# A hybrid decoder step on one core: the V rows of a half step stand behind one half step more of mixer items in TensorE's order

## The chip, the core and the metric

The kernel is one program on one core of a Trainium2 chip. Five engines run at once, each through its own list of instructions in program order, and meet only at semaphores: PE (TensorE, matrix products), DVE (VectorE), ACT (ScalarE), POOL (GpSimd, which here only issues gathers once the recurrence is over) and SP (SyncE, which issues weight loads). The metric is the device time of one execution in microseconds (us), median of the runs.

## The reference

One decoder layer for 512 prompt tokens and 64 sample tokens (8 sequences of 8), width 1024, all float32:

```python
z = x @ w_in + b_in;  u, q, k, v, g_ssm, g_attn = split(z)
y = s5_scan(u, ...);  ga, gb = split(gelu(y) @ w_glu + b_glu);  ssm_branch = ga * sigmoid(gb)
attn_branch = window_attention(rope(q), rope(k), v, sinks) @ w_attn_up
mix = (sigmoid(g_ssm) * ssm_branch + sigmoid(g_attn) * attn_branch) @ w_out
x1 = layer_norm(ALPHA * x + mix)
# PEER: 8 heads, each picks 16 of 16384 experts for every token
h = einsum('nhkd,nd->nhk', peer_u[idx], x1);  a = gelu(h) * gate
x2 = layer_norm(ALPHA * x1 + einsum('nhk,nhkd->nd', a, peer_v[idx]))
```

For each token 128 rows of `peer_u` and 128 rows of `peer_v`, 4 KB each, are fetched from HBM.

## The kernel before, in words

**Tiles.** The tokens are five tiles: tile 0 holds the 64 sample tokens, tiles 1 to 4 hold 128 prompt tokens each. They pass through the expert layer in the order 1, 0, 2, 3, 4 (`ORDER`). A *slot* (t, k) of a tile is one expert choice of all its tokens: one gather of 128 U rows and one of 128 V rows, 512 KB each. Tiles 1 to 4 have 128 slots; tile 0 is folded on 128 partitions and has 64. A *half step* is two slots, the item `("peer", t, c)`, with slots 2c and 2c+1.

**What a slot passes through.** POOL gathers the U row (L663) into a ring; DVE multiplies it with the token and sums (the *dot*, L1462); after four dots ACT applies gelu (L1762), DVE multiplies by the gate (L1431), and ACT makes a diagonal matrix of the four columns (L1754). The V row has been gathered by POOL meanwhile (L672), four slots behind the U row, and is added to the tile's sum either by PE (two matmuls of 512 columns with the diagonal as weights, L1001, four records in the trace) or, for some slots that a planner picks (`rows_on_vector`), by DVE (L1450). The V rows that `("peer", t, c)` uses are 2c-4 and 2c-3.

**What waits for what.** POOL issues in one list: U row q, V row q-4, U row q+1, and so on. Slots are counted through over tiles here (q). A U row waits until the dot of the earlier holder of its place is done, a V row until the earlier holder of its place has been added (`wait_v_used`). For the first 72 slots the V ring has 9 places, from there to the end of tile 0 it has 6 (`V_PLACES`): V row q then waits for V row q-6. Since the list is in order, a V row that waits also holds back all U rows behind it.

**The mixer beside it.** While tiles 1 and 0 are in their slots, the token mixer of tiles 2 to 4 runs in small items between the half steps: `qkv`, `turn`, `s`, `pt`, `pv` (attention), `gs`, `ga` (gates: 8 matmuls with K of 128 each, L896), `merge` (gb, gl and up: 16 such matmuls), `wo` (4 matmuls each, L924), `wo_last` (L934), `xt` (transposes of the normed tile, L944), `wq` (the expert queries, L953) and `sc` (L984). `schedule()` writes out one list of all items; every engine walks it in a version of its own. DVE's and ACT's versions put their share of the mixer items one or two half steps behind (`half_steps_behind`). PE's version is `mixer_first`: it holds each `peer` item back behind the mixer items that follow it, until the next `peer` or `last` item comes.

`rows_on_vector` walks the same two versions with a table of costs, to choose which V rows DVE adds; so the function has two uses.

Of the kernel before, what the change touches and what calls it, by code (L numbers as in the profile page):

```python
# [28 lines left out]
ORDER = [1, 0, 2, 3, 4]  # L29
# [138 lines left out]

def mixer_first(items):


    out, held = [], None
    for item in items:
        if item[0] in ("peer", "last") and held:
            out.append(held)
            held = None
        if item[0] == "peer":
            held = item
        else:
            out.append(item)  # L180
    return out + ([held] if held else [])


def half_steps_behind(items, lag):
# [25 lines left out]
def rows_on_vector(items):  # L210
# [3 lines left out]
    for engine, order in enumerate((half_steps_behind(items, VECTOR_BEHIND), mixer_first(items))):  # L214
        sums, n = [0.0] * (len(steps) + 1), -1 + engine
        for item in order:
            if item[0] == "peer" and item[1] not in ORDER[:2]:
                break
            if item[0] == "peer":
                n += 1  # L220
            elif n >= engine:
                sums[min(n, len(steps))] += COST.get(item[0], (0, 0))[engine]
        load.append(sums)
# [114 lines left out]
def hybrid_step(nc, io):  # L338
# [12 lines left out]
    with ctx:  # L351
# [334 lines left out]
        def _(pe):  # L686
# [334 lines left out]
            for item in mixer_first(plan.items):  # L1021
                if item[0] in here:
                    here[item[0]](*item[1:])
# [866 lines left out]
```

## Time and profile before

| | |
|---|---|
| median of 3 runs | 2079.44 us (2075.89 to 2082.87) |
| the profiled execution, its own time | 2086.46 us |
| its span, first to last instruction | 2084.6 us |
| PE busy | 1600.2 us (77%) |
| DVE busy | 1301.2 us (62%) |
| ACT busy | 442.6 us (21%) |
| POOL busy | 1237.5 us (59%) |
| mean granted TensorE clock | 0.880 |
| HBM | 323 GB/s over the span |

The slots of tile 1 run from 285 us to about 735 us of the span, those of tile 0 from there to about 957 us, those of tiles 2 to 4 take the rest. "Idle before" in a row is the time in which the engine did nothing just before that instruction, and the name behind the arrow is what ended it. A PE row at half clock takes about twice as long. A busy share is an average; which engine holds up a stretch is read from who waits there.

### The profile page before, as it was taken

What the parts mean: (1) busy time and instruction counts of PE and PEld (TensorE: products, weight loads), DVE (VectorE), ACT (ScalarE), POOL (GpSimd) and SP (SyncE); (2) the same over time, 40 slices, a digit from 0 to 9 for tenths busy, and PEclk for the clock granted to TensorE, in tenths of its full rate; (3) what the DMA queues carried; (4) which work ended last, traced back from release to release, by engine and by line L of the source; (5) the groups of instructions that cost most, each with busy time, mean ns of one, the idle gap of its engine ahead of it and who ended that gap; (6) DMA issues with size and microseconds to landing.
All of it is one profiled execution on the core that took longest, in us unless ns stands there. A gap on an engine that the chain in (4) does not pass through costs nothing.

```text
span 2084.6 us, 16770 instructions
## 1 busy us (share of the span) xinstructions
PE 1600.2 (77%) x4829; PEld 811.7 (39%) x4829; DVE 1301.2 (62%) x3093; ACT 442.6 (21%) x1035; POOL 1237.5 (59%) x1370
## 2 busy tenths in 40 slices
PE   7999969798997987974777767577658765777766
PEld 5796655354553432421332323232223322222222
DVE  7820258888888777585786658365758535544345
ACT  2332212354332311111121102111112111111111
POOL 1181027675677657577566667656666675666664
PEclk9999979899998998987888889888888877898987
DMA  6352359997999989899899999989999998999997
GB/s 220 104 156 78 121 209 327 393 342 269 345 405 410 365 329 346 300 351 380 322 342 367 370 371 371 376 313 383 354 368 375 355 393 323 350 369 372 383 377 273
DMA packets 186699, 675.08 MB, mean 324 GB/s; under 512 B 20976, under 2 KB 23456, under 8 KB 186192
## 3 DMA queue, kind: packets, MB, share of 16 engines
q0 software_dynamic: 167056, 609.25, 77.7%
q1 hardware_dynamic: 17632, 59.51, 8.0%
q10 hardware_dynamic: 1920, 5.24, 0.7%
q8 instruction: 40, 0.66, 0.1%
q14 instruction: 51, 0.42, 0.1%
HBM read 669.71 MB, written 3.69 MB: 323 GB/s over the span
## 4 chain that ended last, share of the span: by engine, by line
PE 33%; DVE 20%; POOL 16%; issue 13%; another core or an unknown queue 9%; DMA 7%; ACT 2%; ACTq 0%; POOLq 0%; DVEq 0%; SPq 0%
PE bank L1001 14%; POOL region L672 5%; DVE wring L1462 4%; PE bank L896 4%; POOL region L663 4%; DVE region L1462 4%; POOL wring L663 4%; PE first_banks L896 2%; DMA region<-in_pu,region 2%; DMA wring<-in_pu,region 2%; DMA region<-in_pv,region 2%; PE bank L806 1%; PE bank L713 1%; PE first_banks L806 1%
## 5 line engine op out<-in xcount | busy, mean ns | idle before, releaser
L1001 PE MATMUL bank<-region,small 128*128 128x512 f32 (+1 forms) x1380 | 693.3, 654 | 260.1 <-ACT small L1754 124.0
L672 POOL DMA_INDIRECT region<-in_pv,region x392 | 397.3, 1014 | 250.6 <-issue 104.2
L1001 PEld LDWEIGHTS bank<-region,small 128*128 128x128 f32 (+1 forms) x1380 | 272.4, 204 | 658.2 <-issue 557.8
L663 POOL DMA_INDIRECT region<-in_pu,region x298 | 310.7, 1043 | 194.3 <-issue 84.7
L663 POOL DMA_INDIRECT wring<-in_pu,region x278 | 276.4, 994 | 107.7 <-issue 78.0
L1462 DVE CUSTOM_DVE_ANT_0 wring<-wring,first_banks 128x1024 f32<-128x1024 f32 x228 | 271.7, 1218 | 107.5 <-DMA wring<-in_pu,region 83.0
L1754 ACT ACTIVATE small<-small,region 128x128 f32<-128x128 f32 (+1 forms) x503 | 169.0, 389 | 644.8 <-remote 201.3
L1462 DVE CUSTOM_DVE_ANT_0 region<-region,first_banks 128x1024 f32<-128x1024 f32 x156 | 186.8, 1218 | 72.2 <-DMA region<-in_pu,region 59.9
L1462 DVE CUSTOM_DVE_ANT_0 region<-region 128x1024 f32<-128x1024 f32 x142 | 171.6, 1225 | 38.0 <-DMA region<-in_pu,region 36.5
L1001 PE MATMUL bank<-discretisation,small 128*128 128x512 f32 (+1 forms) x200 | 117.3, 714 | 91.3 <-ACT small L1754 63.3
L1762 ACT ACTIVATE region<-region 128x4 f32<-128x4 f32 x144 | 29.2, 203 | 519.2 <-DVE region L1462 294.6
L1001 PE MATMUL bank<-wring,small 128*128 128x512 f32 x252 | 120.3, 617 | 14.2 <-issue 9.5
L1431 DVE TENSOR_TENSOR region<-region 128x4 f32<-128x4 f32 x144 | 23.1, 161 | 127.6 <-issue 66.1
L1001 PEld LDWEIGHTS bank<-discretisation,small 128*128 128x128 f32 (+1 forms) x200 | 40.2, 213 | 155.0 <-issue 115.8
L1001 PE MATMUL bank<-small 128*128 128x512 f32 (+1 forms) x180 | 93.4, 644 | 7.4 <-issue 6.2
L672 POOL DMA_INDIRECT discretisation<-in_pv,region x60 | 67.1, 1119 | 45.9 <-issue 24.1
L672 POOL DMA_INDIRECT wring<-in_pv,region x64 | 62.2, 971 | 32.6 <-issue 18.8
L1001 PEld LDWEIGHTS bank<-wring,small 128*128 128x128 f32 x252 | 48.4, 197 | 82.4 <-issue 82.0
L1450 DVE SCALAR_TENSOR_TENSOR region<-region 128x1024 f32<-128x1024 f32 x45 | 57.9, 1287 | 33.6 <-issue 25.3
L896 PE MATMUL bank<-xT,wring 128*128 128x192 f32 (+1 forms) x336 | 77.2, 388 | 0.0
L672 POOL DMA_INDIRECT small<-in_pv,region x60 | 61.4, 1023 | 23.2 <-issue 21.8
L1462 DVE CUSTOM_DVE_ANT_0 wring<-wring,region 128x1024 f32<-128x1024 f32 x50 | 60.8, 1222 | 21.3 <-DMA wring<-in_pu,region 20.9
(343 smaller groups left out, 1964.8 us busy)
## 6 DMA issues: line engine op xcount, KB each, us to landing
wring<-in_w SPq DMA_DIRECT2D x100, 512.0 KB, 5.0
region<-in_pv,region POOLq DMA_INDIRECT x392
region<-in_pu,region POOLq DMA_INDIRECT x298
wring<-in_pu,region POOLq DMA_INDIRECT x278
region<-in_w SPq DMA_DIRECT2D x4, 512.0 KB, 6.5
small<-in_small ACTq DMA_DIRECT2D x1, 1669.0 KB, 9.0
xT<-in_xT SPq DMA_DIRECT2D x1, 1536.0 KB, 13.6
region<-in_x SPq DMA_DIRECT2D x3, 512.0 KB
```

The source lines that it names most:

```text
L663: pool.indirect_dma_start(ring_u[u_at.place[q]], None, io["pu"], bass.IndirectOffsetOnAxis(ind[:, k:k + 1], 0)).then_inc(g_u[u_at.place[q] ...
L672: pool.indirect_dma_start(ring_v[v_at.place[q]], None, io["pv"], bass.IndirectOffsetOnAxis(ind[:, k:k + 1], 0)).then_inc(g_v[v_at.place[q] ...
L713: last = mm(b[:, 0:cn], w[:, k, :], xT[:, k, c0:c0 + cn], start=k == 0, stop=k == KT - 1)
L806: last = mm(b[0:tn, 0:n], xT[:, k, t0:t0 + tn], w[:, k % kp, :], start=k == 0, stop=k == KT - 1)
L896: last = mm(b[:, 0:cn], w[:, k0 + k, :], src[:, k, s0:s0 + cn], start=k == 0, stop=k == kn - 1)
L1001: last = mm(bank[6 + hf][0:tn, :], diag[:, d % DIAGS, 0:tn], ring_v[v_at.place[q]][:, 512 * hf:512 * hf + 512], start=k == 0, stop=t > 1 a ...
L1431: V.tensor_tensor(aact[:, n % 2, k], hact[:, n % 2, k], gt[:, k], ALU.mult).then_inc(a_s, 1)
L1450: V.scalar_tensor_tensor(out=acc, in0=ring_v[v_at.place[q]], scalar=aact[:, n % 2, k:k + 1], in1=acc, op0=ALU.mult, op1=ALU.add).then_inc( ...
L1462: V.tensor_tensor_reduce(out=ring_u[u_at.place[q]], in0=ring_u[u_at.place[q]], in1=first_banks[:, :] if t > 1 else x1[t], scale=1.0, scala ...
L1754: S.activation(diag[:, d % DIAGS, 0:tn], eye, ACT.Copy, scale=aact[:, n % 2, k:k + 1]).then_inc(diag_s, 1)
L1762: S.activation(hact[:, n % 2, k], hdot[:, n % 2, k], ACT.Gelu).then_inc(act_s, 1)
```

## The change

`mixer_first` now holds back up to two `peer` items in tiles 1 and 0 (`ORDER[:2]`) instead of one, so that the V rows of half step c stand behind the mixer items of half step c+1 as well. At a `last` item both held ones come out, and from tile 2 on the rule is the old one. No item is added or taken away.

```diff
-    out, held = [], None
-    for item in items:
-        if item[0] in ("peer", "last") and held:
-            out.append(held)
-            held = None
+    out, held = [], []
+    for n, item in enumerate(items):
         if item[0] == "peer":
-            held = item
+            if len(held) == (2 if item[1] in ORDER[:2] else 1):
+                out.append(held.pop(0))
+            held.append(item)
+            while len(held) > 1 and item[1] not in ORDER[:2]:
+                out.append(held.pop(0))
+        elif item[0] == "last":
+            out += held + [item]
+            held = []
         else:
             out.append(item)
-    return out + ([held] if held else [])
+    return out + held
```

The planner's choice moves with it: DVE adds 41 rows of tile 1 instead of 39 (in the first 64 slots rows 3, 7, 11, 12, 13 and 17 instead of 8, 9, 14 and 15; rows 72 and 73 go to PE, 70, 78, 80, 81, 96 and 97 among others to DVE) and 29 of tile 0 instead of 30 (rows 14, 15 and 30 come to DVE, rows 13, 16, 42 and 43 go to PE). The rest of the kernel is the same, 3 lines further down.

PE's list where tile 0 begins its slots, before. L924 is `wo`: rows 1 to 3 of this piece are `wo(0)` (4 matmuls), L1001 with 64x512 is V row (0, 0), and what follows is `wo(1)` and the beginning of `wo(2)`.

```order
L924 MATMUL first_banks<-wring,region 128x512
L924 MATMUL bank<-wring,region 128x512 x2
L924 MATMUL first_banks<-wring,region 128x512
L1001 MATMUL bank<-region,small 64x512 x2
L924 MATMUL first_banks<-wring,region 128x512
L924 MATMUL bank<-wring,region 128x512 x2
L924 MATMUL first_banks<-wring,region 128x512 x2
```

The same place in the changed kernel (L924 is L927 there, L1001 is L1004):

```order
L927 MATMUL first_banks<-wring,region 128x512
L927 MATMUL bank<-wring,region 128x512 x2
L927 MATMUL first_banks<-wring,region 128x512 x2
L927 MATMUL bank<-wring,region 128x512 x2
L927 MATMUL first_banks<-wring,region 128x512
L1004 MATMUL bank<-region,small 64x512 x2
L927 MATMUL first_banks<-wring,region 128x512
```

V row (0, 0) has moved from behind `wo(0)` to behind `wo(1)`, four matmuls later.

PE's list in the middle of tile 0, before: `xt(2)` (L944), V rows 20 and 21, `xt(3)`, rows 22 and 23, `xt(4)`, rows 24 and 25, `wq(1, 0)` (L953), rows 26 and 27.

```order
L944 MATMUL bank<-small,region 128x128 x4
L944 MATMUL first_banks<-small,region 128x128 x4
L1001 MATMUL bank<-discretisation,small 64x512 x2
L1001 MATMUL bank<-small 64x512 x2
L944 MATMUL first_banks<-small,region 128x128 x4
L944 MATMUL bank<-small,region 128x128 x4
L1001 MATMUL bank<-region,small 64x512 x4
L944 MATMUL bank<-small,region 128x128 x4
L944 MATMUL first_banks<-small,region 128x128 x4
L1001 MATMUL bank<-region,small 64x512 x4
L953 MATMUL first_banks<-xT,wring 128x384 x8
```

The same place in the changed kernel (L944 is L947, L953 is L956): `xt(2)`, rows 18 and 19, `xt(3)`, rows 20 and 21, `xt(4)`, rows 22 and 23, `wq(1, 0)`, rows 24 and 25.

```order
L947 MATMUL bank<-small,region 128x128 x4
L947 MATMUL first_banks<-small,region 128x128 x4
L1004 MATMUL bank<-region,small 64x512 x4
L947 MATMUL first_banks<-small,region 128x128 x4
L947 MATMUL bank<-small,region 128x128 x4
L1004 MATMUL bank<-discretisation,small 64x512 x2
L1004 MATMUL bank<-small 64x512 x2
L947 MATMUL bank<-small,region 128x128 x4
L947 MATMUL first_banks<-small,region 128x128 x4
L1004 MATMUL bank<-region,small 64x512 x4
L956 MATMUL first_banks<-xT,wring 128x384 x8
L1004 MATMUL bank<-region,small 64x512 x4
```

Each pair of rows has moved behind one `xt` or `wq` item more: rows 20 and 21 now stand behind `xt(3)`, rows 22 and 23 behind `xt(4)`.

## Rows read from the trace of the kernel before

**Rows 1.** Busy time by stretch: all engines, clock, DMA share, GB/s

```profile
500.00:730.00 230.00, 210.88 (x600) 112.94 (x600) 184.84 (x394) 74.87 (x114) 155.26 (x136) 0.96 0.96 370
730.00:960.00 230.00, 184.95 (x452) 77.19 (x452) 163.13 (x289) 39.47 (x90) 150.24 (x129) 0.90 0.91 332
```

**Rows 2.** Waits of POOL, 285 to 956 us: total, times, longest

```profile
POOL region L672 <- PE bank L1001: 64.7, 20, 15.4
...
POOL region L663 <- DVE region L1462: 28.3, 8, 6.7
```

**Rows 3.** Timeline of PE: last attention item, then the first gate

```profile
500.99 1.93 PE L883 MATMUL first_banks<-region 128*64 128x128 f32 x16 [2.22 <-ACT region L1521]
...
506.39 5.32 PE L896 MATMUL first_banks<-xT,wring 128*128 128x384 f32 x16
```

**Rows 4.** Waits of DVE, 285 to 956 us, on attention items

```profile
DVE region L1253 <- PE bank L873: 7.9, 1, 7.9
...
DVE region L1253 <- PE first_banks L883: 4.2, 1, 4.2
```

**Rows 5.** The page's groups: a V row added by DVE

```profile
L1450 DVE SCALAR_TENSOR_TENSOR region<-region 128x1024 f32<-128x1024 f32 x45 | 57.9, 1287 | 33.6 <-issue 25.3 <-DMA region<-in_pv,region 7.2 <-DVE region L1431 0.4
```

**Rows 6.** Timeline of PE: V rows 74 and 75 of tile 1

```profile
569.96 3.60 PE L1001 MATMUL bank<-region,small 128*128 128x512 f32 x8
```

**Rows 7.** Timeline of POOL: V row 80 and U row 85 issued

```profile
572.12 1.34 POOL L672 DMA_INDIRECT region<-in_pv,region  x1 [3.60 <-PE bank L1001]
573.76 0.94 POOL L663 DMA_INDIRECT region<-in_pu,region  x1 [0.31 <-issue]
```

**Rows 8.** Timeline of DVE: the dot of slot 85

```profile
583.03 1.22 DVE L1462 CUSTOM_DVE_ANT_0 region<-region 128x1024 f32<-128x1024 f32 x1 [3.08 <-DMA region<-in_pu,region]
```

**Rows 9.** Timeline of PE: its stalls late in tile 1

```profile
632.60 5.37 PE L1001 MATMUL bank<-region,small 128*128 128x512 f32 x8 [4.04 <-ACT small L1754]
...
655.96 5.62 PE L1001 MATMUL bank<-region,small 128*128 128x512 f32 x8 [5.96 <-DMA region<-in_pv,region]
...
678.90 6.11 PE L1001 MATMUL bank<-region,small 128*128 128x512 f32 x8 [4.42 <-ACT small L1754]
```

**Rows 10.** Timeline of PE: wo(0), V row (0, 0), wo(1)

```profile
756.72 2.08 PE L924 MATMUL first_banks<-wring,region 128*128 128x512 f32 x2 [6.06 <-DVE region L1283]
...
763.10 1.93 PE L1001 MATMUL bank<-region,small 128*64 128x512 f32 x4
764.96 1.12 PE L924 MATMUL first_banks<-wring,region 128*128 128x512 f32 x2
765.92 1.88 PE L924 MATMUL bank<-wring,region 128*128 128x512 f32 x4
```

**Rows 11.** Timeline of POOL: V row 6 of tile 0

```profile
765.30 0.94 POOL L672 DMA_INDIRECT region<-in_pv,region  x1 [15.41 <-PE bank L1001]
```

**Rows 12.** Timeline of PE: xt(3), rows 22 and 23, xt(4), rows 24 and 25, wq(1, 0)

```profile
831.20 1.09 PE L944 MATMUL first_banks<-small,region 128*128 128x128 f32 x4 [7.68 <-DVE region L1311]
...
833.07 5.77 PE L1001 MATMUL bank<-region,small 128*64 128x512 f32 x8
843.33 0.66 PE L944 MATMUL bank<-small,region 128*128 128x128 f32 x4 [4.49 <-DVE region L1305]
...
844.44 5.21 PE L1001 MATMUL bank<-region,small 128*64 128x512 f32 x8
849.58 5.43 PE L953 MATMUL first_banks<-xT,wring 128*128 128x384 f32 x16
```

**Rows 13.** Timeline of POOL: V rows 28, 30, 34, 36 and 37 of tile 0

```profile
837.01 0.94 POOL L672 DMA_INDIRECT region<-in_pv,region  x1 [4.50 <-PE bank L1001]
...
848.21 1.27 POOL L672 DMA_INDIRECT region<-in_pv,region  x1 [5.44 <-PE bank L1001]
...
866.08 0.94 POOL L672 DMA_INDIRECT region<-in_pv,region  x1 [3.83 <-PE bank L1001]
...
875.01 0.94 POOL L672 DMA_INDIRECT region<-in_pv,region  x1 [4.06 <-PE bank L1001]
...
878.55 0.95 POOL L672 DMA_INDIRECT region<-in_pv,region  x1 [0.30 <-issue]
```

## The prediction

> **What bounds the kernel now.** The change reaches only tiles 1 and 0, the stretch from 285 to about 957 us. I read the busy time by stretch first. From 500 to 730 us PE is busy 211 of 230 us and the DMA engines 0.96 of the time; from 730 to 960 us both are looser, 185 us and 0.91 [rows 1]. So neither is simply the bound. The waits of POOL tell more, since POOL's one list of gathers feeds the whole expert layer: in this part it stood 64.7 us, 20 times, for V rows that PE had not yet added (in one destination buffer alone), against 28.3 us for dots of DVE [rows 2]. The reader is to see that PE's V rows, the very thing that the change moves later, already hold POOL back more than anything else does. Then I followed single places in the timelines: where PE stalls on a diagonal with a mixer item behind it, and where POOL stalls on a V row with a mixer item ahead of it. The first kind gains by the change, the second loses.
>
> **The change part by part.** PE's work is the same: the same matmuls, two or three V rows fewer. What differs is when a V row is added. In a stretch where PE runs without a gap, the mixer items keep their times, and each pair of V rows stands one mixer item later, 5.3 us for a gate [rows 3]. What this costs is read in four places.
>
> *Attention of tile 1, up to 506 us.* Two effects of opposite sign. DVE waited 7.9 and 4.2 us for attention items of PE [rows 4]; with a pair of rows (3.6 us) less ahead of them they could come up to 3.6 us earlier each, 7 us in all. But the last of these items waited itself for ACT's copy, 2.2 us [rows 3], so there the order of PE gives nothing. Against it, DVE adds 6 of the first 64 rows instead of 4, at 1.29 us each [rows 5], and DVE is nearly always busy there: 2.6 us. Bounds: -7 to +5 us (the 2.6 us doubled, if the later rows are late for DVE as well). I take 0, between the ends, since the only one of the two waits whose cause is plain is the one that cannot shrink.
>
> *The stretch without a gap, 506 to 628 us.* At V row 74 the 6-deep ring closes: V row 80 stood 3.6 us until row 74 was added, at 571.8 [rows 7], PE having begun it at 569.96 right behind a `merge` [rows 6]. In the changed list rows 72 and 73 (now on PE, 3.6 us) and the gate `gs(1, 2)` (5.3 us) stand ahead of it: it is added at 569.96 + 3.6 + 5.3 + 1.7 = 580.5, so V row 80 goes out 8.3 to 8.7 us later. U row 85 is the next in POOL's list, and DVE was waiting for just this row: issued at 573.76, its dot begun at 583.03 after 3.08 us of waiting for the landing [rows 7, 8]. So the dots from there on come up to 8.3 us later. PE does not feel it yet, since its own use of the rows is later too. From 628 us on PE has stalls of 4.0, 6.0 and 4.4 us [rows 9]; these it can now fill with mixer items, ACT gets its mixer results sooner and stands less in the way of the diagonals. That gives back something of the 8.3 us, but not what the gathers lost while the DMA engines are 0.96 busy [rows 1]. Bounds 0 and 8.3 us; I take 4, the middle, because the giving back hangs on ACT, which no row here prices.
>
> *Tile 0 begins.* POOL stood 15.4 us until V row (0, 0) was added, then issued V row 6 at 765.30 [rows 11]. PE had done `wo(0)` from 756.72 (after a wait for DVE that the change doesn't touch) and row (0, 0) at 763.10 [rows 10]. Now `wo(1)` comes between. Its four matmuls lie where rows 764.96 and 765.92 begin them: two records by 765.92, four more of 1.88 us and two more, 3.5 us in sum. Everything in POOL's list is behind this, and DVE has run dry: **+3.5 us**. If PE is at half clock there, as it was for `wo(0)`, 7 us; nothing below 3.4.
>
> *The middle of tile 0.* PE reached `xt(3)` at 831.2 after 7.7 us of waiting for DVE, and `xt(4)` at 843.3 after 4.5 us [rows 12]; rows 20 and 21 had been done ahead of the first wait, rows 22 and 23 ahead of the second. Now each pair stands behind it. Counted in the times of before: `xt(4)` ends at 844.4; rows 22 and 23 take 5.2 us at the clock of that moment (as the pair at 844.44 did), `wq(1, 0)` 5.4, rows 24 and 25 3.6, `wq(1, 1)` 5.4, rows 26 and 27 3.6, `wq(1, 2)` 5.4, row 28 1.8: added at 874.8. V row 34 waits for it and was issued at 866.08, 8.7 us earlier [rows 13]. V row 28 goes out at 848 instead of 837.01, V row 30 at 857 instead of 848.21. Row 30 is added by DVE now, so V row 36 no longer waits for PE and comes at POOL's own pace, four gathers of 1.25 us (0.94 and 0.31 between two [rows 7]) behind V row 34: 880 against 875.01. V row 37 waits for row 31, behind row 29, `wq(1, 3)` and its own 1.8 us: 874.8 + 1.8 + 5.4 + 1.8 = 883.8 against 878.55. From there no gather waits for PE. **+5.3 us** stays. Bounds: 0, if the dots of DVE had room for it, and 9, if row 30 doesn't help.
>
> *What is given back.* 53 gathers of tile 0 are left behind V row 37. POOL's mean for one is 1.165 us from 730 to 960 us (150.24 us by 129) [rows 1], while many take 0.94 [rows 7]; at best it regains 0.22 x 53 = 12 us. It would do so only if DVE worked less beside it, and DVE has the same dots and rows to do, later. I take 1 us. A rule of the Trainium skill bears on this (SBUF — State Buffer, section Who interferes with whom): a DVE instruction with two inputs in SBUF blocks a GpSimd instruction that reads SBUF, the later one waiting for the whole of the first. By it a POOL that had been held up, with DVE run dry, would gather at 0.94 us and more of the loss would come back.
>
> The sum is 0 + 4 + 3.5 + 5.3 - 1 = 11.8 us. Tiles 2 to 4 have the old order and shift as a whole; tile 2 begins behind the last gather of tile 0. On the profiled execution, 2086.46 us, this makes 2098.3; that execution lies 7.0 us above the median of the runs, so on the median it is 2079.44 + 11.8 = **2091.3 us**.
>
> **The rivals.**
>
> *Faster: the stalls of PE are filled.* Mechanism: from 628 us on, PE waits with ready mixer items behind it; the three stalls sum to 14.4 us [rows 9]. If the end of tile 1 follows from PE's mixer items, and the loss at row 74 finds slack, 14.4 us come off there, and the losses of tile 0 (8.8 us) are paid from them only in part, if `xt` and `wo` come earlier as well: about 2079.4 - 9 = 2070. It decides once the mixer chain, not the gathers, is what DVE waits for after 628 us. For it: PE's busy 211 of 230 us. Against it: each of these stalls ended on a diagonal or a V landing, so the gathers were behind PE, not PE behind them. A rule of the skill speaks for this rival (Perfetto Trace Analysis, section Optimization Strategies): where the matmul engine idles for others, one should work on keeping it going. Taken as a rule for this kernel it would give the 14.4 us.
>
> *No difference.* The V rows have room: the delays at 572 us and in the middle of tile 0 are swallowed by later waits, and only the 3.5 us at `wo(1)` stay, less what POOL regains. Speaks for it: POOL's waits are many and short, and each may be merely the first of two reasons. 2079 to 2085, say 2082.
>
> *Much slower.* Nothing is given back: 8.3 at row 74, 5 in the attention, 3.5 and 5.3 in tile 0, 22 us: 2101.6. It decides if ACT's diagonals wait for the gathers alone. Speaks for it: the 20 waits of POOL on PE [rows 2], of which I priced three.
>
> *The planner undoes it.* The rows that DVE now takes are others; were they just the ones that close the ring, the order would cost nothing. Row 30 is such a one (counted above), row (0, 0) cannot be, since the first row of a tile is always PE's. This is part of the second rival.
>
> **How the numbers follow.** My forecast (7 to 18 us slower) 0.5; much slower (above 18) 0.12; no difference (-6 to +7 us) 0.22; faster 0.16. About 0.3%, 6.2 us, is what a measurement here tells from no change. So faster 0.16, same 0.22, slower 0.62. The range goes from 2073 (the faster rival's upper part) to 2104 (the much slower one with a little over); it leaves out about 0.1 at the lower end and 0.05 at the upper.
>
> **What the changed profile would show.** Right: POOL's wait for V row 6 of tile 0 is 19 us instead of 15.4; the waits of POOL on PE in sum are longer than before by 15 us or more; PE goes from `xt(2)` to `xt(3)` and `xt(4)` with only a pair of rows between and stands there 10 us and more; PE's stalls between 628 and 680 us are smaller; dots around slot 85 of tile 1 wait for their landing by some 8 us more. Tiles 2 to 4 take the same time from their first dot on. Wrong: if the last dot of tile 1 comes earlier than before, the gathers were not what held the tile, and the first rival is right; if the last dot of tile 0 comes at most 3 us later than before, the second. The weakest step is the 4 us of tile 1.

## The result

| | before | after |
|---|---|---|
| median, 13 runs each on the same chip | 2077.00 us (2062.29 to 2083.46) | 2088.43 us (2075.67 to 2106.57) |
| ratio, 95% interval | | 1.0060 (1.0036 to 1.0083) |
| the profiled execution, its own time | 2086.46 us | 2089.77 us |
| its span | 2084.6 us | 2088.0 us |

The change makes the kernel 12.5 us slower (7.5 to 17.2). Here and below, such a difference and its bounds are worked out from the ratio of the runs; the difference of the two medians can lie up to 2 us beside it. The forecast was 2091.3 us, 11.8 us more than before.

The busy time by stretch of the changed kernel, with the columns of [rows 1]:

```profile
500.00:730.00 230.00, 212.49 (x611) 113.95 (x610) 182.75 (x392) 74.41 (x115) 155.50 (x133) 0.97 0.94 360
730.00:960.00 230.00, 176.96 (x440) 75.33 (x439) 158.53 (x282) 40.56 (x90) 145.81 (x124) 0.89 0.89 322
```

Against [rows 1], POOL has issued 3 instructions fewer in the first stretch (133 for 136) and 5 fewer in the second (124 for 129), and HBM moves 10 GB/s less in both. The gathers have fallen behind while PE has as much to do as before. The waits of POOL, 285 to 956 us, say for what:

```profile
POOL region L675 <- PE bank L1004: 69.3, 20, 17.8
...
POOL discretisation L675 <- PE bank L1004: 21.9, 6, 12.4
POOL region L666 <- DVE region L1465: 15.8, 9, 3.1
...
POOL small L675 <- PE bank L1004: 14.2, 2, 10.0
```

The L675 lines are the three kinds of buffer that V rows land in, 105.4 us together; before they were 64.7 [rows 2], 8.7 and 0.6, 74.0 us together. POOL stands 31 us more for V rows that PE has not added. Not all of it is new waiting: POOL's waits for dots fell from 32.6 us (28.3 [rows 2] and 4.3) to 16.5 (15.8 and 0.7), since a POOL that comes later finds the dots done. Net it waits 15 us more.

V row 80 and U row 85 of tile 1, in POOL's timeline, and the dot of slot 85 in DVE's, answer to [rows 7] and [rows 8]:

```profile
583.15 0.94 POOL L675 DMA_INDIRECT region<-in_pv,region  x1 [3.62 <-PE bank L1004]
584.39 1.54 POOL L666 DMA_INDIRECT region<-in_pu,region  x1 [0.30 <-issue]
```

```profile
594.95 1.22 DVE L1465 CUSTOM_DVE_ANT_0 region<-region 128x1024 f32<-128x1024 f32 x1
```

V row 80 goes out 11.0 us later and the dot of slot 85 starts 11.9 us later. The dot no longer waits for its landing, as my working had it: DVE comes to it late, since the dots ahead of it waited. And V row 80's own wait is 3.6 us, as before: POOL was already late when it came there. It fell behind at V row 59, while the last attention items ran. With 9 places in the ring, V row 59 waits for V row 50. V row 59 in POOL's timeline and V row 50 in PE's, before:

```profile
495.38 0.94 POOL L672 DMA_INDIRECT small<-in_pv,region  x1 [0.30 <-issue]
```

```profile
491.10 1.88 PE L1001 MATMUL bank<-small 128*128 128x512 f32 x4
```

The same in the changed kernel, with U row 64 behind it and the attention items (L886) ahead:

```profile
507.55 1.04 POOL L675 DMA_INDIRECT small<-in_pv,region  x1 [10.03 <-PE bank L1004]
508.90 0.94 POOL L666 DMA_INDIRECT region<-in_pu,region  x1 [0.30 <-issue]
```

```profile
497.54 3.47 PE L886 MATMUL first_banks<-region 128*64 128x128 f32 x16 [6.57 <-ACT region L1524]
...
503.43 1.93 PE L886 MATMUL first_banks<-region 128*64 128x128 f32 x16 [1.40 <-ACT region L1524]
505.29 1.98 PE L1004 MATMUL bank<-small 128*128 128x512 f32 x4
```

V row 50 now stands behind attention items for which PE waits 6.6 and 1.4 us, so V row 59 waits 10.0 us. U row 63 had been 2.4 us later than before; U row 64 is 12.3 us later. The dots had a few rows in hand: they are 2.8 us late at slot 64, wait for landings from slot 68 on, and are 7.7 us late at slot 71. The other traces bear it out. V row 59 waits 9.1 to 10.0 us in all five with this order in tile 1 (`after`, `t1_only`, `order_only`, `order_t1`, `after_again`) and 0.3 us in the nine others. PE's stalls late in tile 1 answer to [rows 9]:

```profile
621.23 3.78 PE L1004 MATMUL bank<-discretisation,small 128*128 128x512 f32 x4 [4.83 <-ACT small L1757]
...
659.29 1.96 PE L1004 MATMUL bank<-discretisation,small 128*128 128x512 f32 x4 [3.16 <-DMA discretisation<-in_pv,region]
...
664.41 3.64 PE L1004 MATMUL bank<-small 128*128 128x512 f32 x4 [3.17 <-DMA small<-in_pv,region]
...
709.40 6.86 PE L899 MATMUL first_banks<-xT,wring 128*128 128x384 f32 x16 [4.14 <-ACT region L1675]
```

They were 14.4 us and are 11.2, with a new one of 4.1 in front of a gate; at the very end of the tile a further one went from 5.8 to 3.3 us. Where tile 0 begins, PE's timeline and POOL's answer to [rows 10] and [rows 11]:

```profile
763.42 2.01 PE L927 MATMUL first_banks<-wring,region 128*128 128x512 f32 x2 [4.10 <-DVE region L1286]
...
772.18 1.93 PE L1004 MATMUL bank<-region,small 128*64 128x512 f32 x4
```

```profile
774.38 0.95 POOL L675 DMA_INDIRECT region<-in_pv,region  x1 [17.78 <-PE bank L1004]
```

V row (0, 0) now stands behind eight matmuls of `wo` and V row 6 goes out at 774.38 instead of 765.30. In the middle of tile 0, PE's timeline (see [rows 12]) and POOL's (see [rows 13]):

```profile
842.63 1.09 PE L947 MATMUL first_banks<-small,region 128*128 128x128 f32 x4 [13.31 <-DVE region L1314]
...
844.50 3.67 PE L1004 MATMUL bank<-discretisation,small 128*64 128x512 f32 x4
```

```profile
848.45 0.94 POOL L675 DMA_INDIRECT discretisation<-in_pv,region  x1 [12.36 <-PE bank L1004]
...
855.07 0.94 POOL L675 DMA_INDIRECT region<-in_pv,region  x1 [1.21 <-PE bank L1004]
...
865.90 1.32 POOL L675 DMA_INDIRECT region<-in_pv,region  x1 [5.22 <-PE bank L1004]
...
883.77 1.43 POOL L675 DMA_INDIRECT region<-in_pv,region  x1 [3.89 <-PE bank L1004]
```

PE waits 13.3 us at `xt(3)` instead of 7.7, with rows 20 and 21 behind it. The rows of POOL are V rows 26, 28, 30 and 34: row 28 goes out 18.1 us later than before, row 30 17.7 us, row 34 17.7 us. By stages, the delay against the profile of before is 6.7 us at the first dot of tile 0, 9.1 at V row 6, 14.7 at V row 37 and 14.5 at the last dot of tile 0. In tiles 2 to 4 this pair of profiles loses part of the difference again, down to 3.4 us at the end; the medians do not, and the section on experiments shows a pair with less scatter in which it stays.

### The profile page after: what moved, and what is told of

Its sections match the earlier page's. It is cut to its first block, busy times and chain, and to the rows that moved or that the text cites. A ratio compares the mean times of both kernels' runs of the same rounds, so it can differ in the third digit from the quotient of the medians.

```text
span 2088.0 us, 16763 instructions
## 1 busy us (share of the span) xinstructions
PE 1610.3 (77%) x4825; PEld 812.7 (39%) x4825; DVE 1300.5 (62%) x3094; ACT 442.1 (21%) x1034; POOL 1239.1 (59%) x1370
## 4 chain that ended last, share of the span: by engine, by line
PE 32%; DVE 26%; issue 13%; POOL 11%; DMA 9%; another core or an unknown queue 6%; ACT 2%; POOLq 0%; DVEq 0%; SPq 0%; ACTq 0%
PE bank L1004 15%; DVE region L1465 5%; DVE wring L1465 5%; DMA region<-in_pu,region 4%; PE bank L899 4%; POOL region L675 3%; POOL region L666 3%; POOL wring L666 2%; PE first_banks L899 2%; DMA wring<-in_pu,region 2%; DMA region<-in_pv,region 2%; PE bank L716 1%; DVE region L1453 1%; PE bank L956 1%
## 5 line engine op out<-in xcount | busy, mean ns | idle before, releaser
L1004 PE MATMUL bank<-region,small 128*128 128x512 f32 (+1 forms) x1356 | 689.8, 658 | 247.3 <-issue 118.1
L675 POOL DMA_INDIRECT region<-in_pv,region x392 | 403.7, 1030 | 242.2 <-issue 108.9
L1004 PEld LDWEIGHTS bank<-region,small 128*128 128x128 f32 (+1 forms) x1356 | 268.7, 206 | 645.5 <-issue 534.6
L666 POOL DMA_INDIRECT wring<-in_pu,region x278 | 274.9, 989 | 106.6 <-issue 77.1
L1004 PE MATMUL bank<-discretisation,small 128*128 128x512 f32 (+1 forms) x200 | 116.3, 711 | 72.5 <-issue 49.0
L1004 PE MATMUL bank<-wring,small 128*128 128x512 f32 x252 | 118.2, 609 | 12.3 <-issue 9.9
L1004 PE MATMUL bank<-small 128*128 128x512 f32 (+1 forms) x200 | 104.0, 646 | 12.0 <-ACT small L1757 4.3
L675 POOL DMA_INDIRECT discretisation<-in_pv,region x60 | 62.7, 1045 | 53.7 <-PE bank L1004 30.2
L1004 PEld LDWEIGHTS bank<-discretisation,small 128*128 128x128 f32 (+1 forms) x200 | 39.3, 211 | 136.9 <-issue 118.6
L675 POOL DMA_INDIRECT small<-in_pv,region x60 | 61.8, 1030 | 43.2 <-PE bank L1004 20.8
L1453 DVE SCALAR_TENSOR_TENSOR region<-region 128x1024 f32<-128x1024 f32 x51 | 65.7, 1288 | 34.3 <-issue 27.0
L675 POOL DMA_INDIRECT wring<-in_pv,region x64 | 61.2, 956 | 39.6 <-issue 16.5
L1004 PEld LDWEIGHTS bank<-wring,small 128*128 128x128 f32 x252 | 48.0, 194 | 77.9 <-issue 76.5
```

The lines of the kernel that those rows point to most:

```text
L666: pool.indirect_dma_start(ring_u[u_at.place[q]], None, io["pu"], bass.IndirectOffsetOnAxis(ind[:, k:k + 1], 0)).then_inc(g_u[u_at.place[q] ...
L675: pool.indirect_dma_start(ring_v[v_at.place[q]], None, io["pv"], bass.IndirectOffsetOnAxis(ind[:, k:k + 1], 0)).then_inc(g_v[v_at.place[q] ...
L1004: last = mm(bank[6 + hf][0:tn, :], diag[:, d % DIAGS, 0:tn], ring_v[v_at.place[q]][:, 512 * hf:512 * hf + 512], start=k == 0, stop=t > 1 a ...
L1453: V.scalar_tensor_tensor(out=acc, in0=ring_v[v_at.place[q]], scalar=aact[:, n % 2, k:k + 1], in1=acc, op0=ALU.mult, op1=ALU.add).then_inc( ...
```

## The experiments

Twelve runs were made, in three sets; each set stands beside its own runs of the kernel before. Set 1 found the kernel before at 2077.31 us (29 runs), as above. Sets 2 and 3 ran on two other chips, which took 1960.08 us (15 runs) and 1960.52 us (19 runs) for it; the last section says where they are faster. Tiles 1 and 0, the subject here, take nearly the same time: in the traces of the kernel before on the first and the second chip, the first dot of tile 0 comes at 735.6 us in both and its last at 950.1 and 947.1. On the third chip there is no trace of the kernel before. "Old DVE rows" means that DVE adds the V rows that it added before the change; "new" means those that the planner picks when it walks the changed order.

### Set 1: which tile, and order or planner

Tile 1 alone and tile 0 alone, each with the planner's choice for it: in `mixer_first` of the changed kernel, `item[1] in ORDER[:2]` becomes

```diff
+ item[1] in ORDER[:1]    # t1_only
+ item[1] == 0            # t0_only
```

> The V rows stand one half step further behind in tile 1 alone; tile 0 has the old order. The theory (POOL's gathers are held by V rows that PE adds later) expects about two thirds of the loss: the last U row of tile 1 and the first of tile 0 are issued 7 to 10 us later than before, and this stays: +7 to +10 us. The rival (the loss of tile 1 is slack that tile 0 swallows, and only tile 0's order costs) expects less than 3 us.

Measured: 2081.23 us, ratio 1.0011 (0.9981 to 1.0041), +2.3 us (-4 to +8.5). The time speaks for the rival, but its bounds hold part of the theory's range, and the trace shows the delay that the theory expected: the first U row of tile 0 goes out 9.8 us later than before, the first dot of tile 0 starts 6.5 us later and its last 6.9 us later. This run doesn't decide.

> The V rows stand one half step further behind in tile 0 alone. The theory expects tile 1 as before, V row 6 of tile 0 2 to 4 us later, some 5 to 7 us more by V row 36, +6 to +9 us at the end of tile 0. The rival (the two losses are one: a late start of tile 0) expects nothing in the middle of tile 0, at most +3 us.

Measured: 2091.61 us, ratio 1.0073 (1.0043 to 1.0102), +15.2 us (9 to 21), at or above the upper end of what the theory expected. More of the loss is made by tile 0's order than by tile 1's, by these two medians. The trace is less plain: tile 1, the same program as before, ended later, so that of the 15.9 us at tile 0's last dot 8.6 stood already at its first, and tile 0 itself took 221.7 us instead of 214.4.

The changed order with old DVE rows, and the old order with new DVE rows. Two copies of the function, old (`one_behind`) and new (`two_behind`); one is given to the planner, the other to PE:

```diff
-    for engine, order in enumerate((half_steps_behind(items, VECTOR_BEHIND), mixer_first(items))):
+    for engine, order in enumerate((half_steps_behind(items, VECTOR_BEHIND), one_behind(items))):   # order_only
+    for engine, order in enumerate((half_steps_behind(items, VECTOR_BEHIND), two_behind(items))):   # planner_only
```

> PE's order as in the changed kernel, but DVE adds exactly the V rows that it added before. The theory (it is the order) expects the whole loss, +10 to +18 us, in the middle of tile 0 more than in the changed kernel, since row 30 is back on PE and V row 36 waits for it. The rival (it is the planner's other choice of rows, with two rows more on DVE early and rows 72 and 73 on PE) expects less than +5 us.

Measured: 2101.01 us, ratio 1.0110 (1.0073 to 1.0147), +22.9 us (15 to 31): the order it is, and more than the theory had.

> PE's order as before, but DVE adds the V rows that the planner picks for the changed order. The theory expects little: -4 to +4 us. The rival (the planner's choice is the loss) expects +8 us or more.

Measured: 2071.65 us, ratio 0.9974 (0.9946 to 1.0002), -5.4 us (-11 to +0.4), not quite told from nothing. By the middle values the order costs about twice what the whole change costs, and the planner's other choice of rows takes something of it back. In its trace that gain is made in tile 0, which takes 203.9 us from its first dot to its last instead of 214.4; its first dot comes 4.8 us later than before, not earlier.

### Set 2: the opposite order

If a late V row is what costs, V rows ahead of their mixer items should gain. PE walks a version in which the `peer` items of tile 0 (or of tiles 1 and 0) are not held back at all:

```diff
-        if item[0] == "peer":
+        if item[0] == "peer" and item[1] not in (0,):      # rows_first_t0; (1, 0) in rows_first_both
             held = item
```

> The kernel before, unchanged, for a second profile. In the run with the new order in tile 0 alone, tile 1 is the same program as before, and yet the first dot of tile 0 came 8.6 us later than in the profile before. If that is what one execution differs from the next, this profile too shows tile 1's end some 3 to 9 us off the first one, and then one profile cannot show tile 1's share of the loss. Tile 0, from its first dot to its last, is expected within 2 us of 214.5 us.

Measured: 1963.13 us, one run with its profile, to have a trace of the kernel before on this chip. The first dot of tile 0 comes at 735.62 us, against 735.63 in the first profile, and tile 0 takes 211.5 us, 3.0 less: both expectations missed. So tile 1's end did not scatter between these two; it does between others. Six traces have the same program in tile 1, and the first dot of tile 0 comes at 735.6 and 744.2 us on the first chip, at 735.6 and 736.0 on the second, at 731.3 and 732.4 on the third.

> The opposite direction in tile 0 alone: PE adds the V rows of a half step ahead of the mixer items of that half step; DVE adds the same rows as before. The theory (POOL waits for V rows that stand behind mixer items) expects POOL's wait before V row 6 of tile 0 to fall from 15.4 us to about 3 to 5, the waits before V rows 28 to 36 to shrink, tile 0 10 to 20 us shorter, and the kernel 8 to 18 us faster than before. The rival (mixer items early are what keeps DVE and PE going, so this order stalls the mixer instead) expects wo, xt and wq later by as much, and +5 us or more.

Measured: 1936.16 us, ratio 0.9879 (0.9853 to 0.9905), **-23.7 us** (-29 to -19), the theory's way and more than it had. POOL's V row 6 of tile 0, in the kernel before on this chip:

```profile
764.13 0.94 POOL L672 DMA_INDIRECT region<-in_pv,region  x1 [14.24 <-PE bank L1001]
```

and with the rows first, POOL's timeline, PE's, and the busy time by stretch:

```profile
753.13 1.18 POOL L686 DMA_INDIRECT region<-in_pv,region  x1 [2.90 <-PE bank L1015]
```

```profile
750.93 1.93 PE L1015 MATMUL bank<-region,small 128*64 128x512 f32 x4
757.06 2.08 PE L938 MATMUL first_banks<-wring,region 128*128 128x512 f32 x2 [4.20 <-DVE region L1297]
```

```profile
730.00:960.00 230.00, 186.65 (x484) 80.22 (x485) 189.34 (x372) 45.88 (x103) 163.45 (x151) 0.92 0.99 381
```

Row (0, 0) is done ahead of PE's wait for DVE, and 11 of the 14 us of POOL are gone. In tile 0 POOL waits 18.4 us for PE's V rows instead of 37.9, and the DMA engines are 0.99 busy at 381 GB/s instead of 0.92 at 336. The lead over the kernel before in these two traces is 13.1 us at U row 18 of tile 0, 23.1 us at V row 32 and 23.5 us at the tile's last dot; it stays 24.0 us to the end. The rival's sign is absent: `wo(0)` starts at 757.06 us against 756.71, and `xt(3)` 9.9 us earlier than before.

> The same in tiles 1 and 0. The theory expects tile 1 up to 5 us shorter as well, so 10 to 20 us faster in all. The rival (in tile 1 PE is the bound and DVE waits for attention items, so these must stand first) expects tile 1 5 to 15 us longer, and the kernel slower than with tile 0 alone.

Measured: 1948.76 us, ratio 0.9945 (0.9924 to 0.9965), -10.8 us (-15 to -7). In tile 1 the same move loses, as the rival expected: the first dot of tile 0 comes 7.0 us later than before. The attention items are what is missing: DVE waits 21.1 us for them (L1267, for `pv`) instead of 4.2, the dot of slot 64 is 19.7 us late, and POOL's waits for dots grow from 33.1 to 57.9 us. Neither earlier nor later is right everywhere.

> V rows first in tile 0 on PE, and DVE adds the rows that the planner picks for the changed order, which alone (with PE's order as before) made tile 0 10.6 us shorter. If the two gains come from different waits, this is 10 to 20 us faster than before and better than rows first with the old choice; if both shorten the same waits (V rows 28 to 37), it is no faster than the better of the two.

Here the planner walks the order of the change under study, not the rows-first one, and picks DVE's rows by it. Measured: 1940.41 us, ratio 0.9905 (0.9880 to 0.9929), -18.6 us (-24 to -14). The new rows do not add to the gain: the second case of the expectation.

### Set 3: the terms of the sum, one by one

The changed order in one part only, old DVE rows everywhere. PE walks a version that holds two `peer` items where the condition is true, one elsewhere:

```diff
+ item[1] == 1                       # order_t1
+ item[1] == 0 and item[2] < 9       # order_t0_wo
+ item[1] == 0 and item[2] >= 9      # order_t0_xt
```

> The new order only in half steps 0 to 8 of tile 0 (the wo items), V rows on DVE as before. The step of the sum to be tested is row (0, 0) behind wo(1): V row 6 issued 3.5 us later, and this stays to the end: +3 to +4 us. The rival (later waits swallow it) expects it gone by V row 28.

Measured: 1963.40 us, ratio 1.0018 (1.0004 to 1.0031), **+3.5 us** (1 to 6). POOL's V row 6:

```profile
763.92 0.95 POOL L690 DMA_INDIRECT region<-in_pv,region  x1 [18.32 <-PE bank L1019]
```

POOL waits 18.3 us instead of 14.2 (V row 5 had gone out 4.3 us earlier in this execution). `order_t0_xt`, which has the old order here and sent out V row 5 nearly as early (744.5 us against 743.4), waits 14.8 us: the 3.5 us at V row 6 are there. That they stay to the end, the trace doesn't show. Counted from the first dot of tile 0, V row 20 goes out 0.2 us and V row 28 0.3 us later than in `before_again`, and tile 0 takes 213.2 us, while three traces with old order and old rows in tile 0 take 208.3, 211.5 and 214.4. This is what the rival expected; against it stands the median alone.

> The new order only from half step 9 of tile 0 on (xt and wq items), V rows on DVE as before, row 30 with them on PE. The step to be tested is that rows 20 to 31 stand behind one xt or wq more. By the working of the prediction V row 34 is 8.7 us late; with row 30 on PE V row 36 waits as well, so here 7 to 10 us stay at the end, against 5.3 with the planner's new choice. The rival (the dots have room) expects under 3 us.

Measured: 1970.92 us, ratio 1.0057 (1.0034 to 1.0079), **+11.2 us** (7 to 16). Its middle is more than the forecast had. The stretch is best read beside `order_t0_wo`, which has the order of before there and whose first dot of tile 0 comes 1.1 us earlier. There first POOL (V row 20, U row 25), then DVE (the dot of slot 25, the begin of tile 3's norm, the second drain of `wo_last(4)`), then PE (`xt(3)`):

```profile
804.14 0.99 POOL L690 DMA_INDIRECT discretisation<-in_pv,region  x1 [1.95 <-PE bank L1019]
805.43 0.94 POOL L681 DMA_INDIRECT region<-in_pu,region  x1 [0.30 <-issue]
```

```profile
814.15 1.21 DVE L1480 CUSTOM_DVE_ANT_0 region<-region 128x1024 f32<-128x1024 f32 x1
815.29 1.41 DVE L1310 BATCH_NORM_STATS2 stat<-region 128x6 f32<-128x512 f32 x2
...
823.25 0.69 DVE L1329 SCALAR_TENSOR_TENSOR region<-region,bank 128x512 f32<-128x512 f32 x1
```

```profile
823.37 0.63 PE L962 MATMUL first_banks<-small,region 128*128 128x128 f32 x4 [2.54 <-DVE region L1329]
```

The same instructions in `order_t0_xt`, and V row 26 last:

```profile
810.08 1.19 POOL L690 DMA_INDIRECT discretisation<-in_pv,region  x1 [6.05 <-PE bank L1019]
811.57 0.95 POOL L681 DMA_INDIRECT region<-in_pu,region  x1 [0.30 <-issue]
...
836.42 1.58 POOL L690 DMA_INDIRECT discretisation<-in_pv,region  x1 [9.48 <-PE bank L1019]
```

```profile
821.37 1.23 DVE L1480 CUSTOM_DVE_ANT_0 region<-region 128x1024 f32<-128x1024 f32 x1 [8.24 <-DMA region<-in_pu,region]
822.52 1.42 DVE L1310 BATCH_NORM_STATS2 stat<-region 128x6 f32<-128x512 f32 x2
...
830.49 0.69 DVE L1329 SCALAR_TENSOR_TENSOR region<-region,bank 128x512 f32<-128x512 f32 x1
```

```profile
830.60 1.08 PE L962 MATMUL first_banks<-small,region 128*128 128x128 f32 x4 [14.48 <-DVE region L1329]
```

Read them as one chain. V row 14 stands behind both halves of `wo_last(4)` instead of the first, so V row 20 goes out 5.9 us later; U row 25, next in POOL's list, 6.1 us later; DVE, in order, stands 8.2 us for it and starts the dot 7.2 us later; the norm of tile 3 and the drains of `wo_last(4)` stand behind that dot in DVE's list and are 7.2 us late, and so is `xt(3)`, which needs the normed tile and the banks that the drains free (the profile names a drain, L1329, since it came last). Behind `xt(3)` now stand V rows 20 and 21, and V row 26 waits 9.5 us for row 20. V row 28 then goes out at 842.13 against 827.19, 15 us later; the delay is still 14.0 us at V row 42 and 13.0 us at the tile's last dot, and stays in tiles 2 to 4. So the delay feeds itself: a late V row holds up a gather, a dot, a mixer item of DVE, a mixer item of PE, and with it the next V row. All this holds for the old DVE rows. The changed kernel gives V rows 14 and 15 to DVE, and there V row 20 waits for nobody (0.3 us in `after` and `after_again`): the first link is missing, and only the wait of V row 26 for row 20 is left (12.4 and 10.7 us).

> PE's new order in tile 1 alone, with the V rows that DVE added before. This takes the order of tile 1 apart from the planner's choice. My sum had +4 us for tile 1 (bounds 0 and 8.3, and -7 to +5 in the attention). The theory (the ring closes at V row 80 and at the attention items) expects tile 1 from its first gather to the first dot of tile 0 4 to 12 us longer and the same loss in the time. The rival (tile 1 has slack, only tile 0 pays) expects within 3 us of before.

Measured: 1968.94 us, ratio 1.0053 (1.0032 to 1.0073), **+10.4 us** (6 to 14). V row 59 waits 9.1 us where the traces of before have 0.3, and the dot of slot 85 comes 11.3 us later than in `before_again`. The first dot of tile 0 is at +5.4 us against that trace, which is of the second chip. `order_t0_wo` and `order_t0_xt`, of the same chip as this run and with the tile 1 of before, have it at -4.3 and -3.2 us. Against those two, tile 1 is 8.6 to 9.7 us longer, near what the medians say. PE's stalls of over 1 us from 560 us on, in `order_t1`:

```profile
656.82 3.78 PE L1019 MATMUL bank<-discretisation,small 128*128 128x512 f32 x4 [11.09 <-ACT small L1772]
...
685.41 5.40 PE L1019 MATMUL bank<-region,small 128*128 128x512 f32 x8 [2.21 <-ACT small L1772]
...
737.47 3.78 PE L1019 MATMUL bank<-region,small 128*128 128x512 f32 x4 [8.47 <-ACT small L1772]
```

and in `order_t0_wo`, with tile 1 as before:

```profile
627.03 5.40 PE L1019 MATMUL bank<-region,small 128*128 128x512 f32 x8 [3.56 <-ACT small L1772]
...
650.35 5.76 PE L1019 MATMUL bank<-region,small 128*128 128x512 f32 x8 [5.88 <-DMA region<-in_pv,region]
...
673.12 6.33 PE L1019 MATMUL bank<-region,small 128*128 128x512 f32 x8 [4.12 <-ACT small L1772]
...
727.80 3.78 PE L1019 MATMUL bank<-region,small 128*128 128x512 f32 x4 [7.07 <-ACT small L1772]
```

PE does run ahead to mixer items and skips the stalls of 3.6 and 5.9 us, and then stands 11.1 us at once. The last row of each fence is the same stall, in front of the last V rows of the tile. With it, all stalls of over 1 us sum to 26.8 us (six, with two of 1.6 at 598.77 and 614.39 and one of 1.8 at 714.11) against 20.6; without it, to 18.3 against 13.6. The stalls are moved, and grow. The dots are later now (by 10.3 us at slot 100), and the diagonals that PE waits for are made from them.

> The changed kernel once more, beside the three. If the parts add up, its loss is that of order_t1, order_t0_wo and order_t0_xt (about 4 + 3.5 + 8.5 = 16 us) less what the planner's new choice gives back (5 to 10 us): +6 to +13 us. If the parts hide each other, it is less than the largest of them.

Measured: 1977.59 us, ratio 1.0091 (1.0067 to 1.0115), +17.8 us (13 to 23). That is above the +6 to +13 expected. The three parts sum to 10.4 + 3.5 + 11.2 = 25.1 us, the order as a whole measured 22.9 in set 1; by this difference the new DVE rows take some 7 us back. Against `before_again` the delay in this trace is 3.9 us at the first dot of tile 0, 7.4 at V row 6, 12.8 at V row 37, 12.1 at the tile's last dot, 12.7 at the first dot of tile 2 and 12.3 at the last dot of tile 4: nothing of it is given back in tiles 2 to 4.

## Why the prediction was right, and where its sizes were off

**What bounds the kernel.** Right. POOL's waits for PE's V rows decide. Moving the rows later added 31 us to them (15 us net of the shorter waits for dots) and 12.5 us to the time; moving those of tile 0 earlier halved them there and took 23.7 us off.

**Attention of tile 1, 0 (-7 to +5).** For the dots within its bounds: counted from the first gather, slot 64 comes 2.5 to 3.0 us later in `order_t1` and `after_again` than in `before_again`. DVE's waits for the attention items (7.9 and 4.2 us before [rows 4]) were 4.5 and 1.7 us after, and did not pay; in `before_again` they were 4.2 us in all, so that even the shrinking may be scatter. But I looked at DVE alone here. What I left out is POOL: V row 59, held by V row 50 behind the attention items, is where tile 1's gathers lose their 10 us.

**The stretch without a gap, 4 (0 to 8.3).** The loss is real, and its place was wrong. The step that failed is "At V row 74 the 6-deep ring closes". V row 80 waits 3.6 us in the trace of before and 3.6 after; it goes out 11.0 us later because the gathers were already 12.3 us late at U row 64. The giving back failed too, "these it can now fill with mixer items": with the old DVE rows the stalls went from 20.6 to 26.8 us. The whole order of tile 1 costs 10.4 us (6 to 14) with those rows, above my 4 and with 8.3 inside its bounds. For tile 1 as it stands in the change the evidence is divided. The time of `t1_only` says +2.3 us (-4 to +8.5), the first dot of tile 0 is 6.7 us late in `after`, 6.5 in `t1_only` and 3.9 in `after_again` (7.1 and 8.2 against the two traces of its own chip). That the planner's other rows make up the difference to 10.4 is not shown: in the trace of `planner_only` their gain lies in tile 0, and tile 1 ends 4.8 us later. The 4 came near the mark, if it did, by luck, since neither the place nor the giving back was right.

**Tile 0 begins, 3.5.** Right for V row 6: its wait grew by 3.5 us, from 14.8 in `order_t0_xt` to 18.3 in `order_t0_wo`. In the profile after it was 17.8 us and not 19, since `wo(0)` itself waited 2 us less for DVE. The time of `order_t0_wo`, +3.5 us (1 to 6), agrees that it stays, but its trace has lost it by V row 20; so the staying is open.

**The middle of tile 0, 5.3 (0 to 9).** In the change it came out: from V row 6 to V row 37 the delay grew by 5.7 us in the first pair of traces and by 5.4 in the second. But the number is the sum of two parts that were both larger than I had them. The order by itself, with row 30 on PE, costs +11.2 us (7 to 16), where my bound was 9. The planner's rows by themselves shorten the same stretch by 6.6 us (from 113.2 to 106.6 in the trace of `planner_only`), where I had counted 3.7 for row 30 (9 less 5.3). The step that is wrong for the order is "Counted in the times of before": I let `xt(3)` and `xt(4)` stay where they were and moved only V rows behind them. They depend on DVE's norm and drains, those on a dot, that on a gather, that on a V row, and V rows 14 and 20, which I did not price, closed the circle. With the old rows that put `xt(3)` 7.2 us later. In the change, rows 14 and 15 are DVE's and the circle stays open; there `xt(3)` comes 11.4 and 12.0 us later in the two pairs, 2.7 and 5.3 us more than the dot of slot 24.

**Given back, 1.** About right: behind V row 37 the delay shrinks by 0.2 us to the last dot of tile 0 in the first pair of traces, by 0.8 in the second, by 0.4 from `order_t0_wo` to `order_t0_xt`. POOL's mean instruction from 730 to 960 us did not get shorter: 139.52 / 121 = 1.15 us in `order_t0_xt`, 146.25 / 130 = 1.13 us in `order_t0_wo`. The rule of the Trainium skill (SBUF — State Buffer, section Who interferes with whom) is seen in single gathers all the same. In the trace of before, from 285 to 956 us, the 28 gathers beside which DVE is idle throughout take 0.94 us each, the 118 that begin during a dot 1.42 us in the mean and up to 2.16, which is 0.94 and a whole dot of 1.22. From 970 us on, where the dot reads the token from PSUM (`first_banks`) and only one input from SBUF, 271 begin during a dot and take 0.94 us. So this trace agrees with the rule. That the mean stays, since the delayed gathers meet the same dots, is likely, not shown.

**The rivals.** The faster one fell: PE did run ahead in tile 1, but its stalls of over 1 us from 560 us to the end of the tile went only from 20.2 to 18.6 us in the change, and grew with the old rows; the gathers, not the mixer, set the end. The rule of the Trainium skill that spoke for it (Perfetto Trace Analysis, section Optimization Strategies) asks to keep the matmul engine going by working on the engines that hold it up. In `order_t1` only PE's own list was reordered, so that other work could fill its stalls; they grew, and tile 1 took 8.6 to 9.7 us longer. No difference fell with the interval. Much slower, 22 us: `order_only` measured 22.9, but that is the order with old rows, of which the rival did not speak. "The planner undoes it" was in part right: it undid some 5 to 7 us, not all. So with the old rows the two terms of tile 1 and the middle of tile 0 were too small by some 12 us together, and the planner's rows, for which I had counted 3.7 us in tile 0 and nothing in tile 1, made up for about half; on the chip of set 3 the change costs 17.8 us. That the forecast lies 0.7 us from the measured loss is partly luck.

**Signs and slips.** Of the signs that I had named, two did not come: dots around slot 85 do not wait longer for their landing, they come late, and tiles 2 to 4 did not take the same time in the first pair of profiles (6.5 us less after). Three slips in the working do not move the result: behind V row 37 48 gathers are left, not 53; PE adds one V row fewer in sum (69 by DVE before, 70 after), not two or three; and 2079.44 + 11.8 is 2091.2.

## What to carry to other kernels

Where one engine issues all gathers in order, a late release of a ring place is paid by everything behind it, so put the releasing work ahead of bulk work that has slack, above all ahead of an instruction on which the engine will wait. In tile 0 that was worth 1.2% over the kernel before (`rows_first_t0`). The right distance differs from stage to stage: in tile 1 V rows later made V row 59 wait 10 us, and V rows earlier made DVE wait 21 us for attention items. When a gather goes out late, look for the first gather that is late, not for the wait that you had in mind: V row 80 waited as long before as after. Before pricing a moved step by the old times of its neighbours, follow whether these neighbours themselves depend, through other engines, on the thing that is moved. When a change also feeds a planner, run order and plan apart: here they had opposite signs. And set traces of other variants with the same program in a stretch beside a pair: the first dot of tile 0 scatters by 8.6 us over two such traces of one chip.

## What the runs showed of the hardware

**Gathers beside dots.** A gather instruction of POOL took 0.94 us beside an idle DVE and 1.42 us in the mean when it began during a dot with both inputs in SBUF; with one input in PSUM the same dot did not lengthen it (0.94 us). The source (L1462) has `x1[t]` as the second input in tiles 1 and 0 and `first_banks` from tile 2 on. U rows that land in `wring` buffers, first from 285 to 956 us, then from 970 to 1900 (behind the bar: busy us, mean ns of one):

```profile
L663 POOL DMA_INDIRECT wring<-in_pu,region x50 | 58.3, 1165 | 27.3 <-issue 14.6 <-PE first_banks L953 8.3 <-DVE region L1462 4.3
```

```profile
L663 POOL DMA_INDIRECT wring<-in_pu,region x193 | 184.1, 954 | 69.7 <-issue 53.6 <-DVE region L1462 15.5 <-remote 0.6
```

**Chips.** The same kernel took 2077 us on one chip and 1960 us on two others. Of the 123 us between the spans of the two traces, 117 lie in tiles 2 to 4. The busy time from 970 to 1900 us, kernel before, first on the first chip, then on the second:

```profile
970.00:1900.00 930.00, 639.10 (x1348) 266.83 (x1348) 556.91 (x1386) 147.12 (x427) 608.79 (x638) 0.85 0.95 361
```

```profile
970.00:1900.00 930.00, 716.25 (x1517) 276.43 (x1516) 612.30 (x1473) 159.24 (x482) 695.89 (x730) 0.94 1.03 409
```

HBM gives 361 GB/s against 409 there, with the DMA engines busy 0.95 and 1.03 of the time, and the first dot of tile 0 comes at 735.6 us on both (at slot 64 of tile 1 they are 5.5 us apart). What makes the chips differ, or whether something else used the memory then, was not found. On the slower one, kernels also scatter by 20 us and more from run to run (2064 to 2091 for the kernel before), so that one pair of profiles can hide or feign a difference of 10 us by its end; the three terms of set 3 were read apart where the kernel before scattered by 14 us (1951 to 1965).
